# A gated delta-rule scan whose output lies with tokens on partitions, with the head norm inside the scan

## The reference, cut to what matters

```python
    def step(state, xs):
        q_i, k_i, u_i, w_i, a_i, g_i = xs
        v_new = u_i - jnp.einsum("bhcd,bhde->bhce", w_i, state)
        o_i = (jnp.einsum("bhcd,bhde->bhce", q_i * jnp.exp(g_i)[..., None], state)
               + jnp.einsum("bhcm,bhme->bhce", a_i, v_new))
        g_last = g_i[..., -1]
        k_dec = k_i * jnp.exp(g_last[..., None] - g_i)[..., None]
        state = state * jnp.exp(g_last)[..., None, None] + jnp.einsum("bhcd,bhce->bhde", k_dec, v_new)
        return state, o_i
...
def rms_norm(x, g):
    xf = x.astype(jnp.float32)
    y = xf * lax.rsqrt(jnp.mean(jnp.square(xf), axis=-1, keepdims=True) + RMS_EPS)
    return (y * g.astype(jnp.float32)).astype(x.dtype)
...
    o = rms_norm(o, gdn_norm_g) * jax.nn.silu(z.reshape(b, l, GDN_HEADS, GDN_DV))
    y_a = o.reshape(b, l, GDN_VW) @ w_gdn_out
```

## Time and profile before

| | us |
|---|---|
| median of three executions (lowest, highest) | 3283.13 (3281.78, 3288.65) |
| the profiled execution's own time | 3287.59 |
| its span | 3284.6 |
| PE busy in it | 2997.3 |
| DVE busy | 1089.7 |
| ACT busy | 987.3 |
| POOL busy | 1162.2 |
| mean granted TensorE clock | 0.94 of 2.4 GHz |

### The profile page before, as it was taken

One profiled execution on the slowest core, in us unless ns is written; L12 is line 12 of the kernel. 1 busy time (PEld: TensorE's weight loads), 2 busy tenths in 40 slices (PEclk: granted clock), 3 DMA queues, 4 the chain that ended last, 5 costly groups with the idle time before them and its releaser, 6 DMA issues. The chain is left out here.

```text
span 3284.6 us, 35626 instructions
## 1 busy us (share of the span) xinstructions
PE 2997.3 (91%) x14286; PEld 2338.2 (71%) x14286; DVE 1089.7 (33%) x1790; ACT 987.3 (30%) x1303; POOL 1162.2 (35%) x379
## 2 busy tenths in 40 slices
PE   8999999998789989889999899877899778989998
PEld 6887687886488767767887678534688535768876
DVE  2110207995554151233110110356410545331101
ACT  3331312234422122324331322144223444143312
POOL 4444433444342125524443344100234110444443
PEclk9999999999899589999999999888899989999999
DMA  4222222343000042212222122300122100222221
GB/s 160 89 102 90 90 90 90 105 144 122 26 1 1 26 166 96 85 52 82 98 101 91 51 90 102 137 3 1 52 90 102 58 23 26 77 77 91 101 90 64
DMA packets 40846, 258.00 MB, mean 79 GB/s; under 512 B 4128, under 2 KB 5536, under 8 KB 13088
## 3 DMA queue, kind: packets, MB, share of 16 engines
q1 hardware_dynamic: 37136, 248.09, 21.0%
q10 hardware_dynamic: 3600, 8.39, 0.7%
HBM read 243.88 MB, written 12.58 MB: 78 GB/s over the span
## 5 line engine op out<-in xcount | busy, mean ns | idle before, releaser
L207 POOL TENSOR_TENSOR weights_lo<-weights_raw,weights_hi 128x2048 fp32r<-128x2048 f32 x201 | 941.3, 4683 | 1590.4 <-ACT weights_hi L198 1590.4
L228 PE MATMUL psum<-x_hi,weights_hi 128*128 128x512 f32 (+1 forms) x2560 | 1010.9, 395 | 98.6 <-DVE x_lo L331 53.3
L229 PE MATMUL psum<-x_lo,weights_hi 128*128 128x512 f32 (+1 forms) x2560 | 1004.2, 392 | 0.0
L230 PE MATMUL psum<-x_hi,weights_lo 128*128 128x512 f32 (+1 forms) x2560 | 1003.0, 392 | 0.0
L228 PEld LDWEIGHTS psum<-x_hi,weights_hi 128*128 128x128 f32 x2560 | 490.2, 191 | 216.3 <-issue 85.9
L198 ACT ACTIVATE weights_hi<-weights_raw 128x2048 fp32r<-128x2048 f32 x202 | 386.6, 1914 | 830.0 <-PE psum L230 724.0
L230 PEld LDWEIGHTS psum<-x_hi,weights_lo 128*128 128x128 f32 x2560 | 490.3, 192 | 101.6
L229 PEld LDWEIGHTS psum<-x_lo,weights_hi 128*128 128x128 f32 x2560 | 491.1, 192 | 98.6
L377 DVE SCALAR_TENSOR_TENSOR arena<-arena,psum 128x512 f32<-128x512 f32 x66 | 45.4, 688 | 557.1 <-PE psum L230 557.1
L228 PE MATMUL psum<-h_hi,weights_hi 128*128 (+1 forms) x528 | 207.1, 392 | 7.3 <-PEq L342 7.3
L229 PE MATMUL psum<-h_lo,weights_hi 128*128 (+1 forms) x528 | 206.6, 391 | 0.0
(11 more groups left out here) (256 smaller groups left out, 3262.8 us busy)
## 6 DMA issues: line engine op xcount, KB each, us to landing
weights_raw<-in_stream SPq DMA_DIRECT2D x202, 1024.0 KB, 4.8
keep_gates<-arena ACTq DMA_DIRECT2D x24, 256.0 KB, 2.0
arena<-keep_gates SPq DMA_DIRECT2D x3, 2048.0 KB, 9.5
arena<-in_na_bias SPq DMA_DIRECT2D x1, 3584.0 KB, 13.0
arena<-in_x_t SPq DMA_DIRECT2D x2, 1024.0 KB, 7.9
keep_x<-arena ACTq DMA_DIRECT2D x1, 2048.0 KB, 8.4
keep_yc<-arena SPq DMA_DIRECT2D x1, 2048.0 KB, 7.0
arena<-keep_yc SPq DMA_DIRECT2D x1, 2048.0 KB, 14.1
```

The lines of the kernel that those rows point to most:

```text
L207: K.nc.gpsimd.tensor_tensor(K.wlo[:, 1 - slot, :, :], K.raw[:, 1 - slot, :, :], K.whi[:, 1 - slot, :, :].bitcast(F32), ALU.subtract).then_ ...
L228: K.nc.tensor.matmul(out, whi, xhi, start=start, stop=False)
L229: K.nc.tensor.matmul(out, whi, xlo, start=False, stop=False)
L230: return K.nc.tensor.matmul(out, wlo, xhi, start=False, stop=stop)
```

## The change

The scan's output is made the other way round: queries or inner products are the weights (64 columns of them), and the state or the values move (128 columns), so that the 64 tokens of a side lie on half of the partitions and the 128 features along the columns. One PSUM bank takes a whole item, and items alternate between banks 2 and 3; `output(x)` waits for the copy of item x - 2 in place of x - 1.

ACT has five instructions for an item in place of one: two squares that sum along the columns (`accum_out`), one reciprocal root of the 128 by 2 sums, and two copies that scale each token by its root. After all items TensorE turns the eight units of 128 by 512 back with 32 transposes, even units first (they hold the first 256 tokens), in six PSUM banks; DVE multiplies each by gain and gate in one instruction per side. The block of the head norm is gone, and the read of the gates is issued at the scan's begin.

```diff
--- before.py
+++ after.py
@@ -1220,6 +1220,8 @@
 
     def by_head(ap):
         return ap.rearrange("p (k s n) -> p k s n", k=2, s=2)
+    finish = [0, 2, 4, 6, 1, 3, 5, 7]
+    TURNED = [0, 1, 4, 5, 6, 7]
     with nc.Block() as blk:
         @blk.vector
         def _(dve):
@@ -1243,6 +1245,16 @@
                     s("scan_state").sem, s("scan_state").n())
                 if x + 1 < len(items):
                     correct(x + 1)
+            dve.wait_ge(s("reloaded").sem, s("reloaded").at(16))
+            for y, u in enumerate(finish):
+                heads, tokens = u - u % 2, slice(NT * CHUNK * (u % 2), NT * CHUNK * (u % 2) + NT * CHUNK)
+                dve.wait_ge(s("scan_turned").sem, s("scan_turned").at(y + 1))
+                turned = K.ps[:, TURNED[y % 6], :].rearrange("p (i s c) -> p s i c", s=2, c=CHUNK)
+                for side in range(2):
+                    z = A[:, heads + side, tokens].rearrange("p (i c) -> p i c", c=CHUNK)
+                    out = A[:, QQ + heads + side, tokens].rearrange("p (i c) -> p i c", c=CHUNK)
+                    last = nc.vector.scalar_tensor_tensor(out, turned[:, side], K.vec("gdn_norm"), z, ALU.mult, ALU.mult)
+                last.then_inc(s("scan_taken").sem, s("scan_taken").n())
 
         @blk.gpsimd
         def _(pool):
@@ -1256,11 +1268,27 @@
 
         @blk.scalar
         def _(act):
+            squares = K.small[:, T1:T1 + 32].rearrange("p (x k) -> p x k", k=2)
+            rstd = K.small[:, T1 + 32:T1 + 64].rearrange("p (x k) -> p x k", k=2)
             for x, (n, g) in enumerate(items):
                 act.wait_ge(s("scan_out").sem, s("scan_out").at(x + 1))
-                out = A[:, TT + 4 * g:TT + 4 * g + 4, CHUNK * n:CHUNK * n + CHUNK].rearrange("p (k s) c -> p s k c", s=2)
-                nc.scalar.activation(out, K.ps[:, 2:4, 0:P].rearrange("p s (k c) -> p s k c", c=CHUNK),
-                                     ACT.Copy).then_inc(s("scan_o").sem, s("scan_o").n())
+                for k in range(2):
+                    last = nc.scalar.activation(W[:, 8 + k, 0:P], K.ps[:, 2 + g, P * k:P * k + P], ACT.Square,
+                                                accum_out=squares[:, x, k:k + 1])
+                last.then_inc(s("scan_sq").sem, s("scan_sq").n())
+                act.wait_ge(s("scan_sq").sem, s("scan_sq").at(x + 1))
+                nc.scalar.activation(rstd[:, x, :], squares[:, x, :], ACT.Abs_reciprocal_sqrt, bias=K.eps(RMS_EPS),
+                                     scale=1.0 / GDN_DK).then_inc(s("scan_rstd").sem, s("scan_rstd").n())
+                act.wait_ge(s("scan_rstd").sem, s("scan_rstd").at(x + 1))
+                for k in range(2):
+                    last = nc.scalar.activation(A[:, TT + unit(x, k), block(x)], K.ps[:, 2 + g, P * k:P * k + P], ACT.Copy,
+                                                scale=rstd[:, x, k:k + 1])
+                last.then_inc(s("scan_o").sem, s("scan_o").n())
+
+        @blk.sync
+        def _(sp):
+            sp.dma_start(A[:, 0:8, :], K.dram["keep_gates"][0:8].rearrange("c p n -> p c n")).then_inc(
+                s("reloaded").sem, s("reloaded").n(16))
 
         @blk.tensor
         def _(pe):
@@ -1285,16 +1313,16 @@
 
             def output(x):
                 n, g = items[x]
-                if x >= 1:
-                    pe.wait_ge(s("scan_o").sem, s("scan_o").at(x))
+                if x >= 2:
+                    pe.wait_ge(s("scan_o").sem, s("scan_o").at(x - 1))
                 for k in range(2):
-                    out = [K.ps[:, 2 + side, CHUNK * k:CHUNK * k + CHUNK] for side in range(2)]
+                    out = [K.ps[rows, 2 + g, P * k:P * k + P] for rows in SIDES]
                     for side in range(2):
-                        nc.tensor.matmul(out[side], head(n, g, k, side), A[:, QQ + unit(x, k), half(x, side)],
+                        nc.tensor.matmul(out[side], A[:, QQ + unit(x, k), half(x, side)], head(n, g, k, side),
                                          start=True, stop=False)
                     for side, rows in enumerate(SIDES):
-                        last = nc.tensor.matmul(out[side], W[rows, g, P * k:P * k + P],
-                                                A[rows, AT + unit(x, k), half(x, side)], start=False, stop=True)
+                        last = nc.tensor.matmul(out[side], A[rows, AT + unit(x, k), half(x, side)],
+                                                W[rows, g, P * k:P * k + P], start=False, stop=True)
                 last.then_inc(s("scan_out").sem, s("scan_out").n())
 
             pe.wait_ge(s("scan_zero").sem, s("scan_zero").at(1))
@@ -1304,6 +1332,16 @@
                 if x + 1 < len(items):
                     new_v(x + 1)
                 output(x)
+            pe.wait_ge(s("scan_state").sem, s("scan_state").at(len(items)))
+            for y, u in enumerate(finish):
+                if y == 4:
+                    pe.wait_ge(s("scan_o").sem, s("scan_o").at(len(items)))
+                if y >= 6:
+                    pe.wait_ge(s("scan_taken").sem, s("scan_taken").at(y - 5))
+                for i in range(NT):
+                    t = slice(P * i, P * i + P)
+                    last = nc.tensor.transpose(K.ps[:, TURNED[y % 6], t], A[:, TT + u, t], K.mat("ident"))
+                last.then_inc(s("scan_turned").sem, s("scan_turned").n())
     K.end_block()
 
 
@@ -1362,12 +1400,6 @@
     phase_gdn_inverse(K)
     phase_gdn_tokens(K)
     phase_gdn_scan(K)
-
-    def reload_z(sp):
-        sp.dma_start(K.A[:, 0:8, :], K.dram["keep_gates"][0:8].rearrange("c p n -> p c n")).then_inc(
-            K.s("reloaded").sem, K.s("reloaded").n(16))
-    phase_head_norm(K, "gdn_norm", [(QQ + h, "mean128", K.vec("gdn_norm"), h) for h in range(8)], 40, after=reload_z,
-                    source=K.A[:, TT:TT + 8, :])
     phase_gdn_out(K)
 
     def load_memory(sp):
```

## The result

The changed kernel takes 3220.61 us (median of four executions, 3217.43 to 3226.05) against 3282.45 (four, 3280.47 to 3288.65) in the same comparison: a ratio of 0.9818, 95% interval 0.9802 to 0.9835. The profiled execution took 3226.05 us, its span 3224.1, at a mean clock of 0.954 (0.94 before).

What follows compares the result with a forecast made beforehand. TensorE, busy throughout the scan at 1.2 GHz, was taken as the bound. Saving 35.6 us in the scan and 12.5 at its end, 48.1 in all, gave a median of 3235 us, range 3224 to 3264.

Steps and rivals of the forecast that it cites:

- What bounds it, and the sign: TensorE bounds the scan, so each microsecond it saves there counts in full; faster at 0.93.
- The clock: In the scan: clock returns from 1.2 to 2.4 GHz within some ten microseconds; the forecast's largest choice.
- rival 1: Clock stays at 1.2 GHz through the whole scan: 25.9 us saved, 3257 us; chance 0.33.
- The switch: In the scan: changing tile shape costs 0.22 us at 2.4 GHz, 0.20 at 1.2, giving items of 2.80 and 4.47.
- rivals 3 and 4: Switches with 64 by 64 tiles cost more: slower, 3296 us at 0.7 each (0.05); no difference at 0.45 to 0.62 (0.02).
- The sum for the scan: First output to last matmul: 82.5 us becomes 46.9, ten of them at 1.2 GHz; 35.6 saved.
- Side by side in one bank: Output's second half (line 1324): both sides run together, four records in 0.63 us at 1.2 GHz, 0.43 at 2.4.
- Rival 2: Line 1324's two sides, writing one bank, run in turn: 41.3 us saved, 3242 us; chance 0.08.
- ACT: In the scan: ACT's norm, 2.5 us per item and at most 3.1, stays hidden; cost 0, at worst 4 us.
- The end: From the scan's last matmul to the next block's first DVE instruction: 20.3 us becomes 7.7, 12.5 saved.
- The next block's clock: At the next block's start: up to 2 us if transposes keep the clock up; taken as 0.
- The sum: Whole kernel: 35.6 in the scan plus 12.5 at its end, 48.1 us saved, median 3235; chance 0.50.

Runs made afterwards that it cites:

- b_warm: Kernel before plus six 128x512 matmuls nobody reads, filling TensorE's pauses at the scan's start: 3249.58 us, ratio 0.9899 to the kernel before.
- swap_only: Kernel before with only the new output shapes, transposes and plain copies; norm block and its gates' read stay behind the scan: 3239.77 us, ratio 0.9869.
- a_wait1: Changed kernel, but output(x) waits for ACT to finish item x-1, as in the kernel before: 3239.82 us, ratio 0.9866 to the kernel before.
- a_mirror: Changed kernel with the output's products ordered queries, inner, inner, queries, so four shape changes per item instead of five: 3219.0 and 3223.89 us.
- a_fill_end: a_mirror plus seven 128x512 matmuls nobody reads behind the transposes: 3226.53 us, ratio 0.9834 to the kernel before.
- a_split: a_mirror plus five unread matmuls behind the transposes, and two of eight units given to ACT and POOL: 3228.47 us, ratio 0.9843.
- a_again: The changed kernel once more without an edit: 3226.3 us (five executions), ratio 0.9829 to the kernel before.
- b_again: The kernel before once more without an edit: 3282.6 us (eleven executions), ratio 0.9997.
- b_gates_early: Kernel before with only the read of the gates moved to the scan's start: 3279.09 us against 3285.85, ratio 0.9980.

## Why the prediction was right and where it was wrong

**What bounds it, and the sign.** Right: each microsecond of PE in the scan counted. PE never waits in the changed scan behind its first matmuls, so ACT, DVE and POOL stayed behind it.

**The clock.** Right in kind, and this was most of the gain (b_warm: 32.5 us). The forecast let ten microseconds pass at 1.2 GHz; it was 3.4 (1057.2 to 1060.6). Its argument, that groups like attention's bring the clock back and the old scan's don't, is borne out by swap_only, which has the new output without the norm, and by a_wait1, which has the old wait. That was a choice at even odds, with rival 1 at 0.33: no row told what in the mix brings the clock back, and no run does. Why the old groups don't, though they hold it, stays open. Rival 1 (3257) is out.

**The switch.** This is the step that failed. I took 0.22 us for a change of shape at 2.4 GHz from one row, line 1282 in the scan's first item. That is right for the change into line 1310's shape (0.64 - 4 x 0.107 = 0.21), but the others cost 0.15 (0.365 - 2 x 0.107) to 0.17 (0.81 for line 1301 and the first 1321, six pairs), as a_mirror confirmed by removing one. At 1.2 GHz, 0.20 was right (0.62 apart). So an item has 2.55 us and not 2.80. One row had stood for five switches. No switch costs more than 0.21 us, into the new shape either, so rivals 3 and 4 are out.

**The sum for the scan.** From the first output (1057.54) to the last matmul's end it takes 40.6 us; forecast 46.9. 15.4 items at 0.25 less are 3.8 us; the short spell at the lower clock (3.1 us of it in this stretch, costing 1.3 and not 3.8) is 2.5. Together 6.3, the whole miss in the scan.

**Side by side in one bank.** I took 0.63 and 0.43; it is 0.62 and 0.365, the same as line 1321, whose two sides differ in columns alone. In the trace the records of line 1324's two sides start 6 ns apart (1064.258 and 1064.264). Rival 2 is out. The Trainium skill's rule ("TensorEngine Tiling (Array Packing)", Gotcha 1: PSUM Pressure), that different row tiles can't use one bank at the same time, doesn't hold for these two tiles, which differ in rows and columns and write different partitions of the bank.

**ACT.** Forecast as hidden at 2.5 us of an item's 2.80, with 0 to 4 us at stake. Hidden, as swap_only shows; its work is 1.6 us (1065.47 to 1067.09). The two squares with their reads of the sum take 0.63 us in place of 1.11: a square takes 273 ns where I allowed 363, and the reads begin before the squares end. The hand-overs that I put at 0.1 each add 0.03 to 0.04, and the two copies take 0.63 in place of 0.73. a_wait1 gives what the cover is worth, 11.9 us.

**The end.** Forecast 7.7, measured 7.4; saved 12.9 against 12.5. DVE's instruction started every 0.40 us (6.36 / 16), and not 0.42. The early gates are 4.3 us of it. The Trainium skill ("TensorE: Matmul & The Clock Gate", Part 4: PE-mode transpose) would have had the clock fall over the transposes; it stayed at 1.00 until 1105.0, over 3.75 us of transposes and 3.1 of the pause behind them. In a_mirror it stayed for 9.0 us, from the first transpose (1095.08) to the next block's first matmul (1104.04). That speaks against the rule, but doesn't decide it: the longest pause of PE that passed at 1.00 without transposes ahead of it is 4.7 us in these profiles, so no run shows what 9 us of pause alone would do. By my sum the lower clock would have cost 0.5 us.

**The next block's clock.** I took 0, with 2 us as a bound that helped to set the low end. a_fill_end shows 0 even where the clock stays up. Behind the stage that profile is the shortest of all, but a_split's, with the clock up at the block's start as well, is 5 us longer there.

**The sum.** 35.6 + 12.5 = 48.1 was forecast; 41.9 + 12.9 and 0.2 ahead of the first output make 55.0. On the median that gives 3283.1 - 55.0 = 3228, inside the range, whose low end had allowed for shorter switches and for a scan wholly at 2.4 GHz. The miss of 14.4 us against 3235 is thus in two parts: 6.9 in the stage, 3.8 of it the switch and 2.5 the spell at the lower clock, and some 7.5 outside the stage. a_again's median, 3226.3, is only 1.8 below 3228. What the range had no term for is the scatter of the code around the stage, though the forecast itself put at 6.6 us what a measurement of this kernel can tell: two medians of four or five executions lie 5.7 us apart for the changed kernel and 4.9 for a_mirror. That the median fell outside the range and not inside it is this scatter.

## What to carry to other kernels

A stretch in which TensorE is busy at half its clock is to be read as two questions: what made the clock fall, and what keeps it from coming back. Try the cheap cure first, a few matmuls that nobody reads in the pause ahead; here they alone gave 33 of 55 us. That no row explains why the clock comes back is a reason to run this before forecasting it. In runs of small matmuls count the changes of tile shape, each with a row of its own kind, and put like shapes together. A norm fits under a scan bound by TensorE if the output has two banks: the second bank was worth 12 us.

## What the runs showed of the hardware that I had not expected

- At 1.2 GHz the old mix of shapes kept PE busy for some 80 us in three profiles (before, b_again, b_gates_early) and the clock stayed down; the same instructions started at 2.4 GHz kept that for the whole scan (b_warm). The new mix got it back after 3.4 us in nine profiles of nine.
- A change of tile shape costs 0.14 to 0.15 us at 2.4 GHz between tiles of 128 by 64 and 64 by 64 (a_mirror), 0.21 into tiles with 64 rows and 128 columns, and about 0.20 at 1.2 GHz (the changed kernel).
- Two tiles of 64 by 64 on opposite rows and columns run at the same time into one PSUM bank: 0.365 us for four records, where the streaming alone would take 0.43 in turn.
- Code that is the same in every kernel scattered by 13 us in 2120 between profiles, and the longer ones had a lower mean clock (0.948 in the shortest, 0.941 in the longest).
